# A hybrid diffusion step: the first modulation summed tile by tile, its weights laid out by tile, and x put ahead of them in the weight queue

## What is computed

```
def layer(x, cond, l, p, ctx):
    mod = jnp.einsum('...d,de->...e', jax.nn.silu(cond), p['w_ada'][l]) + p['b_ada'][l]
    sh1, sc1, g1, sh2, sc2, g2 = jnp.split(mod, 6, axis=-1)
    hn = rmsnorm(x, p['norm_mix'][l]) * (1.0 + sc1) + sh1
    mix, ctx_tensors = token_mixers(hn, l, p, ctx)
    x = x + g1 * mix
    hn = rmsnorm(x, p['norm_ffn'][l]) * (1.0 + sc2) + sh2
    x = x + g2 * moe(hn, l, p)
```

## Time and profile before

| | |
|---|---|
| median of 3 runs | 964.01 us (962.23 to 964.07) |
| the profiled execution | 962.35 us, of which the span of the trace is 960.0 |
| PE busy | 925.7 us (96%) |
| DVE busy | 431.9 us (45%) |
| ACT busy | 158.6 us (17%) |
| HBM read | 300.10 MB, 315 GB/s over the span |

### The profile page before, as it was taken

One profiled execution on the slowest core, in us unless ns is written; L12 is line 12 of the kernel. 1 busy time (PEld: TensorE's weight loads), 2 busy tenths in 40 slices (PEclk: granted clock), 3 DMA queues, 4 the chain that ended last, 5 costly groups with the idle time before them and its releaser, 6 DMA issues.

```text
span 960.0 us, 13408 instructions
## 1 busy us (share of the span) xinstructions
PE 925.7 (96%) x5205; PEld 500.9 (52%) x5205; DVE 431.9 (45%) x780; ACT 158.6 (17%) x408; POOL 63.6 (7%) x96
## 2 busy tenths in 40 slices
PE   6999999999999999999999999999989999999996
PEld 2755575668554444344437556557865444443442
DVE  1386887743422213222235999676252321222322
ACT  1212024321210001000111201442021001000100
POOL 1113130020000000000010223000000000000001
PEclk9899999999999999999999999999999999999998
DMA  9997564685999999999995622510189999999992
GB/s 366 395 390 266 214 265 181 241 305 191 421 417 420 421 422 421 421 423 421 420 420 219 227 89 89 201 69 28 45 354 421 422 420 421 422 421 421 422 419 104
DMA packets 48430, 303.63 MB, mean 316 GB/s; under 512 B 7680, under 2 KB 7696, under 8 KB 14960
## 3 DMA queue, kind: packets, MB, share of 16 engines
q1 hardware_dynamic: 42368, 291.52, 74.7%
q0 software_dynamic: 2960, 8.63, 2.6%
q10 hardware_dynamic: 3040, 2.62, 0.8%
HBM read 300.10 MB, written 2.65 MB: 315 GB/s over the span
## 4 chain that ended last, share of the span: by engine, by line
PE 85%; DVE 10%; ACT 2%; DMA 2%; issue 1%; SPq 0%; DVEq 0%; ACTq 0%
PE ps L427 83%; PE ps L461 2%; DMA ring<-in_w_ada 2%; ACT eP L1573 1%; DVE rt L1050 1%; DVE fa L1256 1%; DVE sq L1207 1%; DVE hnT L1098 1%; DVE xy L1250 1%; DVE stat L1050 1%; DVE x L1556 0%; DVE proj L1217 0%; DVE t L1295 0%; DVE proj L1283 0%; DVE nsq L1554 0%
## 5 line engine op out<-in xcount | busy, mean ns | idle before, releaser
L427 PE MATMUL ps<-ring,proj 128*64 128x512 f32 x1024 | 226.3, 595 | 1.0 <-ACT proj L1818 1.0
L427 PE MATMUL ps<-ring,hnT 128*128 128x512 f32 (+1 forms) x576 | 202.1, 503 | 1.8 <-DVE hnT L1429 0.8
L427 PEld LDWEIGHTS ps<-ring,hnT 128*128 128x128 f32 x576 | 106.4, 190 | 74.0 <-issue 64.0
L427 PEld LDWEIGHTS ps<-ring,proj 128*64 128x64 f32 x1024 | 72.6, 137 | 132.8 <-issue 131.1
L427 PE MATMUL ps<-hnT,ring 128*64 128x128 f32 (+2 forms) x576 | 75.8, 346 | 1.5 <-DVE hnT L1098 1.5
L427 PEld LDWEIGHTS ps<-hnT,ring 128*64 128x64 f32 (+1 forms) x576 | 61.5, 163 | 14.1 <-issue 2.2
L427 PEld LDWEIGHTS ps<-proj,xs 128*128 128x128 f32 x512 | 58.4, 192 | 12.5 <-issue 11.4
L427 PE MATMUL ps<-proj,xs 128*128 128x128 f32 x512 | 61.4, 278 | 0.1
L427 PE MATMUL ps<-proj 128*128 128x512 f32 x128 | 61.5, 606 | 0.0
L1545 DVE COPY proj<-ps 128x512 f32<-128x512 f32 x16 | 11.1, 692 | 108.1 <-PE ps L427 108.1
L427 PE MATMUL ps<-ring,silT 128*32 128x512 f32 x384 | 49.3, 635 | 10.0 <-DVE silT L1066 6.9
(11 more groups left out here) (231 smaller groups left out, 926.3 us busy)
## 6 DMA issues: line engine op xcount, KB each, us to landing
ring<-in_w_gate SPq DMA_DIRECT2D x64, 1024.0 KB, 14.5
ring<-in_w_down SPq DMA_DIRECT2D x64, 1024.0 KB, 17.1
ring<-in_w_ada SPq DMA_DIRECT2D x48, 1024.0 KB, 8.6
ring<-in_w_in SPq DMA_DIRECT2D x28, 1024.0 KB, 8.0
eP<-in_w_up SPq DMA_DIRECT2D x16, 1024.0 KB, 16.2
wT<-in_w_up SPq DMA_DIRECT2D x16, 1024.0 KB, 18.3
fa<-in_w_up SPq DMA_DIRECT2D x16, 1024.0 KB, 18.1
xy<-in_w_up SPq DMA_DIRECT2D x16, 1024.0 KB, 19.6
```

The source lines that it names most:

```text
L427: ins = nc.tensor.matmul(*a, **k)
```

## The change

The modulation of layer 0's first normalization is no longer summed over rows of `w_ada` for all 2048 columns at once. The host lays its weights out as `ada_x`: eight slices of 1 MB, each with all 1024 rows for the shift and scale columns of one tile of 128 features. `sums_of_feature(k)` makes the whole sum of one tile with eight matmuls (four 32-wide places, two each), ACT copies 256 columns, `modulation_of_feature(k)` turns them with two small matmuls, DVE and ACT finish tile k of `hnT`, and `feature_of_first_block(k, ...)` at once adds tile k's products into the two banks of block f. The two slots of f are loaded behind the first and the fourth slice (`ROWS_AHEAD`), and stay taken until the tiles 0 to 3 and 4 to 7 are done. cond, the two halves of x and the first constants are issued by SP ahead of the weights instead of by POOL. The eight later steps that stood behind f, q and a (2, 3, 3) now all stand behind a's fourth quarter, four ahead of the two `diagonal`s and four behind them.

```
-ADA_BEHIND = ((2, 3, 3, 3, 3, 2, 3, 2), (0, 0, 0, 0, 0, 3, 0, 0))
+ADA_BEHIND = ((0, 0, 8, 3, 3, 2, 3, 2), (0, 0, 0, 0, 0, 3, 0, 0))
 AT_CHANGE = 5
+ROWS_AHEAD = (1, 4)
...
+            for name, dst, src in (("cond_dma", condT[:], ap["cond"]), ("x_dma0", x[:, 0], ap["x_prompt"][0]),
+                                   ("begin_dma", C["begin"][:], ap["begin"]), ("x_dma1", x[:, 1], ap["x_sample"][0])):
+                sp.dma_start(dst, src).then_inc(S(name), 16)
...
                 if l == 0:
-                    for step in EARLY:
-                        load_ada(*step)
+                    for k in range(KC):
+                        if k in ROWS_AHEAD:
+                            load_rows(*IN_BLOCKS[0], ROWS_AHEAD.index(k))
+                        load(flat_slot, ap["ada_x"][k])
...
+                def sums_of_feature(k):
+                    pe.wait_ge(S("bank1_free"), c.claim(1))
+                    s = slot()
+                    for i in range(KC):
+                        q = slice(32 * (i % 4), 32 * (i % 4) + 32)
+                        last = mm(ps[q, 1, 0:2 * P], silT[:, i, :], by_k(s, 2 * P)[:, i] if i < KH else flat_slot(s)[:, 2 * P * i:2 * P * (i + 1)], start=i < 4, stop=i >= 4)
...
+                def modulation_of_feature(k):
+                    pe.wait_ge(S("bank7_free"), c.claim(7))
+                    pe.wait_ge(c.of("modX", 0, 0, k), c.at("modX", 0, 0, k))
+                    for a in range(2):
+                        last = mm(ps[:, 7, NG * a:NG * (a + 1)], modX[:, 2 * P * (k % 2) + P * a:2 * P * (k % 2) + P * (a + 1)], C["pick"], start=True, stop=True)
...
+                def feature_of_first_block(k, ss, banks):
+                    for g in range(NG):
+                        pe.wait_ge(c.of(f"hn1S{g}", k), c.at(f"hn1S{g}", k))
+                    for p in range(2):
+                        for hl in range(2):
+                            for d in range(2):
+                                col = 64 * (2 * p + hl) + 256 * d
+                                last = mm(ps[64 * d:64 * d + 64, banks[p], 256 * hl:256 * (hl + 1)], by_k(ss[k // KH], 512)[:, k % KH, col:col + 64], hnT[:, k, :], start=False, stop=(k == KC - 1), skip_group_check=True)
...
+                    f_banks = [next_bank() for _ in range(2)]
+                    pe.wait_ge(c.of("zero", 0), c.at("zero", 0))
+                    stream_zeros(f_banks[0], 8)
+                    pe.wait_ge(c.of("silT"), c.at("silT"))
+                    sums_of_feature(0)
+                    stream_zeros(f_banks[0], 3)
+                    stream_zeros(f_banks[1], 2)
+                    pe.wait_ge(c.of("begin_dma", 0), c.at("begin_dma", 0))
+                    normalized_group("hn1", "xn1", 0, banks=(4, 5))
+                    normalized_group("hn1", "xn1", 1, banks=(6, 0))
+                    ss = []
+                    for k in range(KC):
+                        modulation_of_feature(k)
+                        if k + 1 in ROWS_AHEAD:
+                            ss.append(slot())
+                        if k + 1 < KC:
+                            sums_of_feature(k + 1)
+                        feature_of_first_block(k, ss, f_banks)
+                        if k % KH == KH - 1:
+                            owed.append(ss[k // KH])
...
                     for k in range(KC):
-                        ins = ts(hnT[:, k, 0:P], hnT[:, k, 0:P], modT[:, 1, k, 0:1], modT[:, 0, k, 0:1], ALU.mult, ALU.add)
+                        dve.wait_ge(c.of("modT", 0, 0, k), c.at("modT", 0, 0, k))
```

More of the change, by code:

```diff
@@ L70, in host_constants @@
     at = [(32 * (2 * a + h), g) for h in range(2) for a in range(2) for g in range(NG)]
+    c["pick"] = np.stack([t % 32 == g for g in range(NG)], 1)
     c["pickm"] = np.stack([t == row + g for row, g in at], 1)
@@ L333, in build @@
         ADA = {"x": (0, 1), "g": (2, 5), "y": (3, 4)}
-        EARLY = [(0, "x", k) for k in range(KC)]
         LATER = [[(0, "g", k) for k in range(KC)] + [(0, "y", k) for k in range(KC)] + [(1, "x", k) for k in range(KC)],
@@ L482, in claim_for_norm, with normalized_group @@
                 return b
-            def normalized_group(stage, factors, g, ahead=None, first=None):
+            def normalized_group(stage, factors, g, ahead=None, banks=(None, None)):
                 xv = x[:, g].rearrange("p (k q) -> p k q", k=KC)
                 for h in range(2):
-                    b = claim_for_norm() if h or first is None else first
+                    if banks[h] is None:
+                        b = claim_for_norm()
+                    else:
+                        b = banks[h]
+                        pe.wait_ge(S(f"bank{b}_free"), c.claim(b))
                     if not h:
@@ L553, in at_change @@
                         ada_step(*step)
[L555 to L566, removed]
+                def sums_of_feature(k):
[4 more added lines that the diff above has]
+                        last = mm(ps[q, 1, 0:2 * P], silT[:, i, :], by_k(s, 2 * P)[:, i] if i < KH else flat_slot(s)[:, 2 * P * i:2 * P * (i + 1)], start=i < 4, stop=i >= 4)
+                        if i < KC - 1:
+                            pay(last)
+                    last.then_inc(c.fills(1, "ada", 0, "x", k), 1)
+                    owed.append(s)
@@ new lines, in modulation_of_feature @@
+                def modulation_of_feature(k):
[3 more added lines that the diff above has]
+                        last = mm(ps[:, 7, NG * a:NG * (a + 1)], modX[:, 2 * P * (k % 2) + P * a:2 * P * (k % 2) + P * (a + 1)], C["pick"], start=True, stop=True)
+                        if not a:
+                            pay(last)
+                    last.then_inc(c.fills(7, "modT", 0, 0, k), 1)
@@ new lines, in feature_of_first_block @@
+                def feature_of_first_block(k, ss, banks):
[6 more added lines that the diff above has]
+                                last = mm(ps[64 * d:64 * d + 64, banks[p], 256 * hl:256 * (hl + 1)], by_k(ss[k // KH], 512)[:, k % KH, col:col + 64], hnT[:, k, :], start=False, stop=(k == KC - 1), skip_group_check=True)
+                                if k == KC - 1 and hl and d:
+                                    last.then_inc(c.fills(banks[p], "projP", "f", p), 1)
+                                else:
+                                    pay(last)
@@ L598, in by_head_and_group @@
                     for g in range(NG):
-                        if l and g:
+                        if g:
                             normalized_group("hn1", "xn1", 1)
@@ L786, in ada_behind @@
                     ada_steps(ADA_BEHIND[l]["fqabirvs".index(name)])
[L788 to L793, removed]
+                if l:
+                    b = next_bank()
+                    ss = open_block("f")
+                    by_head_and_group("f", 0, ss, b)
+                    by_head("f", 1, ss)
+                else:
+                    f_banks = [next_bank() for _ in range(2)]
[18 more added lines that the diff above has]
+                            owed.append(ss[k // KH])
                 ada_behind("f")
@@ L801, in _ @@
                 b = by_token("a", 1, 0, ss)
+                if not l:
+                    by_token("a", 1, 1, ss, b)
+                    ada_steps(ADA_BEHIND[l][2] // 2)
                 diagonal(0)
                 diagonal(1)
-                by_token("a", 1, 1, ss, b)
-                ada_behind("a")
+                if l:
+                    by_token("a", 1, 1, ss, b)
+                    ada_behind("a")
+                else:
+                    ada_steps(ADA_BEHIND[l][2] // 2)
                 ss = open_block("b")
@@ L1837, in _ @@
             g_ = nc.gpsimd
[L1838 to L1843, removed]
+            pool.dma_start(mods[:], ap["mods"]).then_inc(S("mod_dma"), 16)
+            led.made("mod_dma", ("mod_dma",), 16)
             for l in range(L):
@@ L1957, in laid_out @@
     w_out = np.asarray(inputs["w_out"]).reshape(L, D, 2, BLK).transpose(0, 2, 1, 3)
+    first = np.asarray(inputs["w_ada"])[0, :, 0:2 * D].reshape(P, KC, 2, KC, P)
+    out["ada_x"] = first.transpose(3, 0, 1, 2, 4).reshape(KC, P, KC * 2 * P)
     out["w_out"] = halves(w_out, KH).reshape(L, 2, 2, P, KH * BLK)
```

47 lines of the change are left out of this document (27 added, 20 removed).

## The result

The changed kernel took 970.38 us (median of 4 runs, 969.54 to 971.92), the kernel before beside it 963.27 us. The ratio is 1.0077, with a 95% interval of 1.0063 to 1.009: 7.1 us slower, where 2.6 were forecast. The direction was right, but the size lies outside the range. The profiled execution took 969.54 us, its span 967.7 (960.0 before).

The account below looks back on a forecast made before the run. PE bounds the kernel (85% of the span). T comes 4.5 us sooner, but the ring starts b 0.8 later; with 1.8 for the clock, +2.6 on 962.35 gives 964.9 profiled, median 966.6 us; range 959.5 to 970.

Parts of the forecast that it names:

- T: End of block f on PE, 48.94 us before; forecast 44.4, 4.5 us sooner, between 43 and 47.
- the contention in the ring: SP's eleven transfers behind T, slowed by POOL's parameters: 4.5 us of their 6.6 us DMA time falls beside them.
- the round: One round of f's loop: 1.6 us chain, 1.68 us products, 0.05 weight loads; 3.35 us, eight rounds 26.8.
- other slots are no limit: Ring behind T: slot of a's second half is free by T + 21.4, the queue reaches it at T + 28.
- The first sums: Front part, ahead of the loop: x and first slice land, sums, zeros, transposes; loop starts at 17.6 us, up to 19.
- The ring: Behind T: a's second half waits for f's slot; b's second half lands at T + 35.6, PE idles 5.4 us.
- DVE: Gates' chain behind T: `hq` comes at T + 24.7, PE at T + 24.5; cost 0.2 us, at most 1.
- The clock: Behind the wait ahead of b the clock falls: 1.8 us lost, between 0 and 3.4.
- A short wait or a kept clock (1): Wait at b short or clock kept: b starts at 78 to 81, time within 0.2% (1.9 us); chance 0.29.
- the clock did not stay low in the loop (3): Rival: clock stays low in f's loop, round 5.9 us, T at 65, 14 to 20 us lost, about 982; chance 0.03.
- Rival 2: Transfers come ahead of PE at b: b starts at 74.6, 4.6 us sooner, 959.4 us; chance 0.22.

Follow-up runs that it names:

- kept: Changed kernel with matmuls on constants, results unused, giving PE work ahead of a (28) and b (25): 969.72 us, ratio 1.0072.
- params_q: Changed kernel with POOL's parameters issued behind block q instead of behind block f: 971.19 us, ratio 1.0091.
- params_early: Changed kernel with POOL's parameters issued behind tile 5 of the loop, f's slots still in the ring: 965.15 us, ratio 1.0018.
- own_late: own_early with POOL's parameters back behind f: 965.09 us, ratio 1.0023.
- own_early: Changed kernel with f in two spare buffers, the ring's turn kept, and POOL's parameters issued at tile 5: 965.86 us, ratio 1.0028.
- own_apart_q: own_early with later steps 2, 3, 3 behind f, q and a, diagonals behind a's last quarter, parameters behind q: 960.15 us, ratio 0.9974.
- own_slots: Changed kernel with f's halves in two spare buffers, shifting the ring's turn by two: 983.27 us, ratio 1.0199.
- before_grouped: Kernel before, with only the later steps and the diagonals placed as in the changed kernel: 965.06 us, ratio 1.0019.

## Why the prediction was right in direction and wrong in size

From the profiles (us; a dash is no wait):

| kernel | f's halves | parameters | T | wait at a | first late step | b starts | wait at b | ratio |
|---|---|---|---|---|---|---|---|---|
| changed | ring | behind f | 46.2 | 3.67 | 72.67 | 85.17 = T + 38.9 | 3.31 | 1.0077 |
| kept | ring | behind f | 47.6 | filled | 72.35 | 86.83 = T + 39.2 | filled | 1.0072 |
| params_q | ring | behind q | 47.5 | - | 68.39 | 86.72 = T + 39.2 | 3.10 | 1.0091 |
| params_early | ring | tile 5 | 48.2 | - | 69.06 | 81.45 = T + 33.2 | 3.20 | 1.0018 |
| own_late | spare | behind f | 46.6 | - | 67.43 | 79.81 = T + 33.2 | 3.19 | 1.0023 |
| own_early | spare | tile 5 | 48.1 | - | 68.98 | 81.36 = T + 33.2 | 3.19 | 1.0028 |
| own_apart_q | spare, steps apart | behind q | 46.9 | - | | 77.53 = T + 30.7 | 0.51 | 0.9974 |

It falls into three levels. With f's slot in the ring and the parameters behind T, b starts at T + 39 wherever in between the parameters stand and whether a waits or not: that is DMA time (from 52 to 85 us the DMA engines of the changed kernel have no rest). Take away either one, and it is T + 33.2 in all three kernels (in own_slots too), always 12.4 us behind the first of the eight steps: that is the grouping, with 11.0 us in before_grouped, where the last landing is 1.4 us shorter. In the changed kernel b starts 12.5 us behind that step, since the wait and the low clock at a had made the step late: there both limits end together. kept and params_q, at 14.5 and 18.3 us behind it, show DMA time alone. Undo the grouping with f in spare buffers, and it is T + 30.7: 30.2 of PE's own work and a wait of 0.51. The two causes of the first level are not added: each alone costs nothing measurable beyond the grouping, together 5 us.

Two terms of the prediction's sum were too small, the contention in the ring (4.5 us taken, 8.0 measured) and the round (3.35 taken, 3.61 measured), and its "other slots are no limit" was wrong. By its steps:

**The first sums** were right: the loop began at 17.36 us, forecast 17.6. Other profiles of the same front had 17.7 to 19.4; the first slice landed there 0.4 to 1.3 us later; so T was 46.2 to 48.2. That 17.36 came so near to the forecast is in part luck of this one profile.

**The round** was mis-sized: 3.61 us, forecast 3.35. The mechanism was right: it is the chain over DVE and ACT, and then f's products. The chain took 1.74 us (1.6 taken), f's products 1.88 (1.68 taken, as a quarter of a row of other shapes), and the 0.05 for weight loads did not show. The tile's sums lie beneath the chain, as forecast; the view of PE prints no idle time there, since with 0.13 us it is below the 0.15 that this view shows, but the eighth round, without sums, takes as long to its products as the second. That is 0.26 x 8 = 2.1 us, which less the 0.2 of the earlier start makes T's 1.8: the gain at T was 2.7 us instead of 4.5, and by the other profiles 0.7 to 2.3.

**The ring** was right in what waits: a's second half went out at T + 0.7 (T + 1.0 forecast), for f's slot. Its size was wrong, T + 38.9 instead of T + 35.6, and the term that failed is the contention: 4.5 us were taken, and 8.0 measured. The first transfer took 10.0 us, 5.0 more than alone, and the ten behind it 85.1 - 57.0 = 28.1 us, not 25.1. I had let 2.1 of the parameters' 6.6 us of DMA time pass ahead of SP's first transfer. POOL's first issue stands at 45.75 and SP's at 46.96, 1.2 us apart, and the parameters' packets took 49.3% of the 14 us from 46 to 60, 6.9 us; so nearly all of it fell beside SP's transfers. Of the other 1.1 us, 0.8 are the late landing of b's second half (3.3 us behind the first, see own_late); and a slot takes 2.54 us rather than the 2.51 of the forecast, whose first transfer was issued at 50.02 and not 50.1. This term is the larger part of the miss, 3.3 us. The trace of before had such an overlap, which I overlooked: at the start, with x on POOL's queue beside them, the first three slices landed 3.8 us apart, the last four 2.5.

**"Other slots are no limit"** was wrong, and I had looked at only one slot. The eight steps fill all eight slots, and b's halves need those of the first two, which are free only when PE has run these steps: issued at 69.4 and 70.2 in own_late, 1.9 and 2.8 us behind the first step, the second landing at 79.7. In the changed kernel DMA time hid this limit; b waits 3.2 us and loses 1.7 to 2.8 us by the clock as soon as the first loss is mended. before_grouped shows it as a cost of its own, 1.82 us of wait without the clock.

**A wait at a** was not foreseen. My own terms held it: the slot's transfer at T + 6 plus 4.5 of contention, against PE at T + 7.1. It delayed nothing that the transfers to b did not delay as well (kept).

**DVE** was right: `hq` was done at 70.49, T + 24.3, and the diagonals waited for nothing.

**The clock** was right: 5.37 against 3.70 behind b, 1.67 us lost, 1.8 forecast. That it would also fall behind a was not foreseen, as the wait there was not.

So b began 6.0 us later than in the earlier trace rows instead of 0.8: 1.8 from T, 3.3 from the landing. With the clock that is 7.7 in the span.

**The rivals.** A short wait or a kept clock (1) did not occur, and the clock did not stay low in the loop (3). Rival 2, transfers ahead of PE, is what own_apart_q made true; it gave 960.15 and not 959.4, since T is later than I had it. By the Trainium skill, DMA: Bandwidth & Descriptors, section Issuing engines are not separate DMA queues, transfers of all issuers run on the same 16 engines and interleave: the trace agrees, with 10.0 us for a landing of 5.0 beside POOL's. The Trainium skill, TensorE: Matmul & The Clock Gate, section HAM oscillation, tells of a kernel whose loop waits for a transfer in every round, longer than it computes, and starts each round at half rate. The loop here is no such case: its pauses are 0.13 to 0.20 us, 1.13 in the last round, and it doesn't test this. params_q comes nearest: its late steps wait for a transfer each, and behind the idle times of 2.31 and 1.45 us a step took 1.94 us instead of 1.06, which agrees.

**Open.** Why the first slice lands at 9.7 us in one profile and up to 11.0 in others was not tried, nor what makes the landing of b's second half up to 1.4 us longer in some kernels than in before_grouped. What the clock behind b alone is worth in the total stays between 0 and 1.7 us, since kept had a later T.

## What to carry to other kernels

Follow each slot of a ring to its next user, and each transfer ahead of a block back to the slot that it needs: a buffer held over a long loop costs nothing until the transfer behind it has no lead, and a group of as many steps as there are slots takes the lead from the block behind it. Two things that each cost nothing alone can cost 5 us together, so undo them singly and in pairs, and read the place in the trace, since an edit's side effect elsewhere (own_slots) can hide its gain. Moving other traffic later within the same stretch only moves the wait; moving it to where the DMA engines idle takes it away.

## What the runs showed of the hardware

Between 52 and 60 us the DMA engines were busy for 0.99 of the time but moved only 356 GB/s, while the parameters were among their packets, and 420 from 78 to 85: the parameters' 2.19 MB took 6.9 us of all engines' time (46 to 60 us), where 420 GB/s would make 5.2. An idle time of 1.82 us on PE (before_grouped) left the clock up, as did 1.16 us behind work on constants (kept); idle times of 3.19 us and more (changed, own_late, own_early) brought it to 0.50. In params_q it was at 0.50 from 81 us on, behind idle times of 2.31 and 1.45 us, and stayed there over the next, of 3.10. The loss behind the same 3.19 us was 1.65 us in own_early and 2.8 in own_late.
